# Three gathers of a decoder block leave out the rows of one or two DMA engines; a 48-partition gather brings them, and their steps go last

## The chip, the cores and the metric

The kernel runs on one core of one Trainium2 chip. A core has five engines that run their own instruction streams: TensorE (PE), VectorE (DVE), ScalarE (ACT), GpSimd (POOL) and SyncE (SP). Sixteen DMA engines move data between memory (HBM) and the on-chip SBUF. The metric is the device time of one execution in microseconds; three runs of the kernel before gave a median of 930.43 us (929.78 to 933.73).

## The reference

One layer of a decoder block on 256 tokens of width 1024: an adaptive norm, two attention branches, and a feed-forward part (PEER) that looks up experts. The last part is what matters here. For each token and each of 8 heads the 16 best of 16384 experts are found; each has a row `u` and a row `v` of 1024 numbers.

```python
def one_chunk(args):
    xc, ec, gc = args
    ue = u[ec]
    ve = v[ec]
    act = jax.nn.gelu(jnp.einsum("cd,chkd->chk", xc, ue), approximate=False)
    return jnp.einsum("chk,chkd->cd", (gc * act).astype(ve.dtype), ve)
```

That is 256 x 8 x 16 pairs of rows, 268 MB in float32, gathered from HBM by number. The result is added to the block's stream, and a last norm gives the output.

## The kernel before, in words

The first 237 us load weights and compute the norms and attention for all tokens (for the second half of the tokens the rest of it runs later, between the steps below). Then the expert part runs as 256 steps g, in blocks of 16 (`BLOCK`): one block for each of 8 heads, first for tokens 0 to 127 (steps 0 to 127), then for tokens 128 to 255. In a step each of the 128 partitions is a token, and the step handles one expert of each token. A row of the table `uv` holds `u` and `v` side by side, 2048 float32 or 8 KB.

- POOL issues gather g (L929): an indirect DMA that takes one row number per partition from column g of `expert` and brings 128 rows of 8 KB into slot `SLOT[g]` of eleven. Before it POOL waits until the step that used the slot last (`OLD[g]`) is through: for all late steps that is PE's count `v_used`. At the first gather of a block it also waits for the block's row numbers (`eid_ready`, L1686). The gathers use one semaphore per slot, 16 counts per gather.
- DVE waits for the landing and multiplies the `u` half with the token's row, summing into one number (`dot`, L1711, two instructions).
- ACT makes the step's factor from it (`diagonal`: L1156 the activation, L1165 the gate, L1169 a diagonal 128x128 matrix with the factor).
- PE multiplies that matrix with the `v` half into the sum in PSUM (`value_step`, L808, four matmul instructions of 512 columns in each step, with their weight loads) and counts `v_used`.
- Beside the steps of a block, DVE finds the next block's experts (`halves_first` to `expert_sums` at places 3 to 9 of the block, `normalize` at 11), and ACT its gates (`gate_exponent` at 8).

All engines go through the steps in the same order, 0 to 255. The last two steps (`LAST`, 254 and 255) are gathered in halves of 4 KB: first both `u` halves (L936), then both `v` halves (L939). Step 254 isn't done by PE: DVE multiplies its `v` half by factor and gate (L1830) and adds it to the stream (L1831). Then DVE takes PE's sum in two halves of 512 columns (L1837, L1838; the first half waits for `first_half_done`, set by PE after the first half of step 255), ACT squares and sums them (L1173), and after the root (L1248) DVE scales the rows (L1718) and SP writes them out.

Of the kernel before, what the change touches and what calls it, by code (L numbers as in the profile page):

```python
# [74 lines left out]
for _n, _w in (("ident", P), ("cmask", T), ("cos", TT * HALF), ("sin", TT * 2 * HALF),  # L75
               ("cmp_add", TT * NCMP), ("cmp_mul", TT * NCMP), ("bmask", HEADS), ("pos", NCAND)):
    TAB[_n] = (_at, _at + _w)
    _at += _w
# [48 lines left out]
def transpose_jobs():  # L127
# [18 lines left out]
    for r in (4, 5, 6, 7, 8, 9):  # L146
# [29 lines left out]
EARLY, MORE, MOST = 36, 64, 127  # L176
SLOT = [(0, 1, 2, 3, 4, 5, 6, 9, 10)[g % 9] if g < EARLY else (g - EARLY) % 7 if g < MORE else (7, 8, 0, 1, 2, 3, 4, 5, 6)[(g - MORE) % 9] if g < MOST else
        (9, 10, 7, 8, 0, 1, 2, 3, 4, 5, 6)[(g - MOST) % 11] for g in range(STEPS)]
USE = [SLOT[:g].count(SLOT[g]) for g in range(STEPS)]
OLD = [max((i for i in range(g) if SLOT[i] == SLOT[g]), default=None) for g in range(STEPS)]  # L180

# [3 lines left out]
ON_PE = [v for v in range(STEPS) if v not in ON_DVE and v != STEPS - 2]  # L185
# [17 lines left out]
def build(nc, A, out):  # L203
    with ExitStack() as ctx:
# [25 lines left out]
        last_rows = sb("last_rows", 2 * len(LAST), P, U32)  # L230

# [171 lines left out]
        first_half_done, last_ready, last_amount = sem("first_half_done"), sem("last_ready"), sem("last_amount")  # L403
        last_u = [sem(f"last_u{i}") for i in range(len(LAST))]
# [77 lines left out]
        def _(pe):  # L482
# [317 lines left out]
            def value_step(v):  # L800
# [4 lines left out]
                if v in LAST:  # L805
                    pe.wait_ge(uv_in[SLOT[v]], 16 * (USE[v] + 1))
# [46 lines left out]
            for g in range(STEPS + 1):  # L853
# [3 lines left out]
                if g - 1 in PE_NO and g - 1 >= EARLY_STEPS:  # L857
                    value_step(g - 1)
# [48 lines left out]
        def _(pool):  # L907

            for g in range(STEPS):
# [33 lines left out]
        def _(act):  # L943
# [248 lines left out]
            for g in range(STEPS):  # L1192
                b, i = divmod(g, BLOCK)
                if g >= EARLY_STEPS:
                    diagonal(g)
# [4 lines left out]
                if i == 8 and b + 1 < BLOCKS:  # L1200
# [50 lines left out]
        def _(dve):  # L1251
# [429 lines left out]
            def expert_sums(b, lo, hi):  # L1681
# [5 lines left out]
                dve.wait_ge(eid_ready, b + 2 if b else 1 + lo // 4)  # L1687
                if b == BLOCKS - 1:
# [13 lines left out]
            def dot(g):  # L1702
# [5 lines left out]
                else:  # L1708
                    dve.wait_ge(uv_in[SLOT[g]], 16 * (USE[g] + 1))
# [61 lines left out]
            for g in range(STEPS):  # L1771
# [3 lines left out]
                dot(g)  # L1775
# [173 lines left out]
```

## Time and profile before

| | |
|---|---|
| median of 3 runs | 930.43 us (929.78 to 933.73) |
| profiled execution, its time | 930.88 us |
| its span, first to last instruction | 929.1 us |
| PE busy | 775.1 us, 83% |
| DVE busy | 654.0 us, 70% |
| ACT busy | 413.7 us, 45% |
| POOL busy | 285.8 us, 31% |
| DMA, all bytes | 342.33 MB, mean 368 GB/s over the span |
| first gather issued, last one | 237.3 us, 899.5 us |
| mean granted TensorE clock | 0.98 |

All views come from one execution, the profiled one. Busy shares are means over the whole span; the gathers run in the last three quarters of it. "DMA share" is the time of the DMA packets that begin in a stretch, divided by sixteen engines' time in that stretch; it can come out a little over 1. Times in rows are microseconds from the start of the span unless marked ns; a bracket at the end of a row gives the idle time of the engine before the instruction and what ended it.

### The profile page before, as it was taken

What the parts mean: (1) busy time and instruction counts of PE and PEld (TensorE: products, weight loads), DVE (VectorE), ACT (ScalarE), POOL (GpSimd) and SP (SyncE); (2) the same over time, 40 slices, a digit from 0 to 9 for tenths busy, and PEclk for the clock granted to TensorE, in tenths of its full rate; (3) what the DMA queues carried; (4) which work ended last, traced back from release to release, by engine and by line L of the source; (5) the groups of instructions that cost most, each with busy time, mean ns of one, the idle gap of its engine ahead of it and who ended that gap; (6) DMA issues with size and microseconds to landing.
All of it is one profiled execution on the core that took longest, in us unless ns stands there. A gap on an engine that the chain in (4) does not pass through costs nothing.

```text
span 929.1 us, 9674 instructions
## 1 busy us (share of the span) xinstructions
PE 775.1 (83%) x2880; PEld 418.6 (45%) x2880; DVE 654.0 (70%) x1697; ACT 413.7 (45%) x1157; POOL 285.8 (31%) x262
## 2 busy tenths in 40 slices
PE   4999999998978897897787798778687777877785
PEld 3445778888724453354444364323222222222221
DVE  4534669974798879867666868685966757576656
ACT  3112222342568789342424543564634344353433
POOL 0000000000444344553333445525354252543430
PEclk8999999999999999999999999999899999999999
DMA  9967249660799999999999999999999999999993
GB/s 362 423 260 328 91 158 378 279 273 23 284 423 420 420 393 393 424 420 417 419 420 419 420 418 423 420 422 421 421 424 420 422 422 420 422 420 423 422 420 152
DMA packets 47619, 342.33 MB, mean 368 GB/s; under 512 B 5392, under 2 KB 6608, under 8 KB 11088
## 3 DMA queue, kind: packets, MB, share of 16 engines
q0 software_dynamic: 37152, 268.45, 69.8%
q1 hardware_dynamic: 9968, 72.79, 19.6%
q10 hardware_dynamic: 448, 0.48, 0.2%
q8 instruction: 23, 0.38, 0.2%
q14 instruction: 28, 0.23, 0.1%
HBM read 340.65 MB, written 1.05 MB: 368 GB/s over the span
## 4 chain that ended last, share of the span: by engine, by line
DMA 44%; PE 30%; DVE 13%; ACT 4%; issue 4%; POOL 3%; SPq 0%; POOLq 0%; DVEq 0%
DMA extra<-in_uv,arena 27%; DMA arena<-in_uv,arena 13%; PE banks L808 7%; PE banks L562 6%; PE banks L516 5%; DVE extra L1711 3%; PE banks L525 3%; POOL extra L929 3%; DMA extra<-in_uv,last_rows 2%; PE banks L778 2%; PE banks L759 2%; DMA extra<-in_w_ada 2%; PE banks L747 2%; DVE arena L1711 1%; DVE arena L1730 1%
## 5 line engine op out<-in xcount | busy, mean ns | idle before, releaser
L929 POOL DMA_INDIRECT extra<-in_uv,arena x132 | 150.1, 1137 | 430.2 <-DVE arena L1759 236.9
L808 PE MATMUL banks<-extra 128*128 128x512 f32 x472 | 231.4, 619 | 58.7 <-ACT extra L1169 57.7
L808 PE MATMUL banks<-arena,extra 128*128 128x512 f32 x312 | 156.3, 626 | 40.6 <-ACT extra L1169 40.6
L1156 ACT ACTIVATE arena<-arena 128x1 f32<-128x1 f32 x256 | 51.6, 202 | 305.3 <-DVE arena L1711 304.8
L808 PEld LDWEIGHTS banks<-extra 128*128 128x128 f32 x472 | 82.4, 191 | 184.2 <-ACT extra L1169 114.0
L929 POOL DMA_INDIRECT arena<-in_uv,arena x84 | 93.9, 1118 | 135.3 <-PE banks L808 58.5
L1711 DVE CUSTOM_DVE_ANT_0 extra<-extra 128x1024 f32<-128x1024 f32 x75 | 91.6, 1225 | 36.4 <-DMA extra<-in_uv,arena 35.2
L808 PEld LDWEIGHTS banks<-arena,extra 128*128 128x128 f32 x312 | 54.5, 192 | 130.4 <-ACT extra L1169 84.9
L1711 DVE CUSTOM_DVE_ANT_0 extra<-extra,arena 128x1024 f32<-128x1024 f32 x59 | 72.2, 1225 | 43.7 <-DMA extra<-in_uv,arena 43.1
L1169 ACT ACTIVATE extra<-tab,arena 128x128 f32<-128x128 f32 x234 | 93.9, 401 | 7.7
L808 PE MATMUL banks<-ring,extra 128*128 128x512 f32 x152 | 74.4, 616 | 20.6 <-ACT extra L1169 20.4
L1711 DVE CUSTOM_DVE_ANT_0 arena<-arena 128x1024 f32<-128x1024 f32 x45 | 55.1, 1225 | 37.3 <-DMA arena<-in_uv,arena 36.8
L1165 ACT ACTIVATE arena<-arena 128x1 f32<-128x1 f32 x234 | 68.9, 294 | 7.6
L1711 DVE CUSTOM_DVE_ANT_0 arena<-arena,extra 128x1024 f32<-128x1024 f32 x39 | 47.6, 1225 | 15.2 <-DMA arena<-in_uv,arena 14.6
L808 PEld LDWEIGHTS banks<-ring,extra 128*128 128x128 f32 x152 | 26.5, 191 | 63.3 <-ACT extra L1169 41.3
L929 POOL DMA_INDIRECT ring<-in_uv,arena x38 | 36.9, 970 | 45.8 <-PE banks L808 28.7
L562 PE MATMUL banks<-arena,extra 128*128 128x256 f32 x192 | 46.0, 394 | 0.8 <-ACT arena L1035 0.5
L516 PE MATMUL banks<-arena 128*128 128x512 f32 (+1 forms) x96 | 42.8, 604 | 3.2 <-ACT arena L980 3.2
L1711 DVE CUSTOM_DVE_ANT_0 ring<-ring,arena 128x1024 f32<-128x1024 f32 x24 | 29.4, 1225 | 18.9 <-DMA ring<-in_uv,arena 18.6
L562 PEld LDWEIGHTS banks<-arena,extra 128*128 128x128 f32 x192 | 36.7, 196 | 6.5 <-issue 1.6
L1156 ACT ACT_TABLE_LOAD x30 | 38.5, 1283 | 0.5
L778 PE MATMUL banks<-arena 128*128 128x128 f32 x256 | 33.6, 288 | 3.7 <-ACT arena L1111 3.7
(280 smaller groups left out, 1044.7 us busy)
## 6 DMA issues: line engine op xcount, KB each, us to landing
arena<-in_w_ada SPq DMA_DIRECT2D x6, 2048.0 KB, 8.4
arena<-in_w_late SPq DMA_DIRECT2D x24, 512.0 KB, 8.2
extra<-in_w_ada SPq DMA_DIRECT2D x6, 1024.0 KB, 17.1
extra<-in_w_gate SPq DMA_DIRECT2D x3, 2048.0 KB, 8.3
extra<-in_w_in SPq DMA_DIRECT2D x2, 2048.0 KB, 31.6
extra<-in_w_ada SPq DMA_DIRECT2D x2, 2048.0 KB, 9.8
extra<-in_w_br SPq DMA_DIRECT2D x2, 2048.0 KB, 9.2
arena<-in_w_wq SPq DMA_DIRECT2D x2, 2048.0 KB, 14.5
```

The lines of the kernel that those rows point to most:

```text
L516: last = nc.tensor.matmul(B[2 * c + tt][:, 0:CHUNK_COLS[c]], hT[:, k, tt * P:(tt + 1) * P], first[:, k, c0:c0 + CHUNK_COLS[c]], start=(k = ...
L525: last = nc.tensor.matmul(B[2 * (c - FIRST) + tt][:, 0:CHUNK_COLS[c]], hT[:, k, tt * P:(tt + 1) * P], w[:, k, :], start=(k == 0), stop=(k ...
L562: last = nc.tensor.matmul(B[6 if m else 1][:, 0:T], w[:, k, (m % 4) * P:(m % 4 + 1) * P], hT[:, k, :], start=(k == 0), stop=(k == KT - 1))
L747: last = nc.tensor.matmul(merge_bank[tt][m // 2 % 2][:, (2 * (m % 2) + b) * P:(2 * (m % 2) + b + 1) * P], wb[b][:, k, :], oT[:, b, k, :], ...
L759: last = nc.tensor.matmul(B[m % 2][:, 0:P], w[:, k, :], hT[:, k, tt * P:(tt + 1) * P], start=(k == 0), stop=(k == KT - 1))
L778: last = nc.tensor.matmul(B[m % 2][:, 0:P], w[:, k, :], h2[:, k, tt * P:(tt + 1) * P], start=(k == 0), stop=(k == KT - 1))
L808: last = nc.tensor.matmul(acc[tt][:, half * 512:(half + 1) * 512], diag[i % DIAGS], uv_slot[SLOT[v]][:, D + half * 512:D + (half + 1) * 51 ...
L929: nc.gpsimd.indirect_dma_start(uv_slot[SLOT[g]], None, A["uv"], bass.IndirectOffsetOnAxis(ap=expert[:, g:g + 1], axis=0)).then_inc(uv_in[S ...
L1156: link(nc.scalar.activation(gel[:, v:v + 1], dots[:, v:v + 1], ACT.Gelu))
L1165: link(nc.scalar.activation(amount[:, v:v + 1], gel[:, v:v + 1], ACT.Copy, scale=weight[:, v:v + 1]))
L1169: nc.scalar.activation(diag[i % DIAGS], ident, ACT.Identity, scale=amount[:, v:v + 1]).then_inc(diag_ready, 1)
L1711: V.tensor_tensor_reduce(out=row, in0=row, in1=h2row[g // FIRST_HALF], scale=1.0, scalar=0.0, op0=ALU.mult, op1=ALU.add, accum_out=dots[:, ...
```

## The change

Three gathers, of steps 233, 234 and 235 (`APART`), are told not to fetch some rows: a number of 1048576 (`SKIP`) is added to the row numbers of the partitions concerned, and the gather has a bounds check that passes over numbers beyond the table. Left out are the eight partitions that its formula `engine_rows` gives for DMA engine 3 (12 to 15 and 44 to 47), for step 235 also those of engine 1 (4 to 7 and 36 to 39). A second gather for each, over partitions 0 to 47 alone (`NARROW`), issued by POOL right after gathers 244, 245 and 246, fetches what was left out and passes over the others; POOL waits before it for the first part's landing. The row numbers for both come from two new DVE instructions when block 14's experts are known, with a table of 6 new columns.

The steps 233 to 235 are processed by DVE, ACT and PE after step 253 and before 254 (`ORDER`). Their three slots aren't used again, so that from gather 236 on eight slots go round. Block 15's experts and gates are found three places earlier in block 14, by the count of steps processed. `LANDED` replaces the count of uses in the waits for a landing. The core of the diff:

```diff
+APART = (STEPS - 23, STEPS - 22, STEPS - 21)
+APART_SECOND = {STEPS - 12 + i: c for i, c in enumerate(APART)}
+AHEAD = len(APART)
+NARROW = 48
+SKIP = 1 << 20
+def engine_rows(e):
+    return [p for p in range(P) if 8 * (p >> 6) + ((p >> 2) & 7) == e]
+APART_ROWS = (engine_rows(3), engine_rows(3), engine_rows(1) + engine_rows(3))
...
-        (9, 10, 7, 8, 0, 1, 2, 3, 4, 5, 6)[(g - MOST) % 11] for g in range(STEPS)]
+        (9, 10, 7, 8, 0, 1, 2, 3, 4, 5, 6)[(g - MOST) % 11] for g in range(APART[-1] + 1)]
+SLOT += [SLOT[APART[0] - 11 + AHEAD + i % (11 - AHEAD)] for i in range(STEPS - len(SLOT))]
+LANDED = [16 * sum(1 + (i in APART) for i in range(g + 1) if SLOT[i] == SLOT[g]) for g in range(STEPS)]
+ORDER = [c for c in range(STEPS - 2) if c not in APART] + list(APART) + [STEPS - 2, STEPS - 1]
...
-                if g - 1 in PE_NO and g - 1 >= EARLY_STEPS:
-                    value_step(g - 1)
+                if g - 1 >= EARLY_STEPS and ORDER[g - 1] in PE_NO:
+                    value_step(ORDER[g - 1])
...
+                if g in APART:
+                    i = 2 * APART.index(g)
+                    pool.wait_ge(apart_ready, 1)
+                    nc.gpsimd.indirect_dma_start(uv_slot[SLOT[g]], None, A["uv"],
+                                                 bass.IndirectOffsetOnAxis(ap=apart_rows[:, i:i + 1], axis=0),
+                                                 bounds_check=KEYS * KEYS - 1, oob_is_err=False).then_inc(uv_in[SLOT[g]], 16)
+                    continue
...
+                if g in APART_SECOND:
+                    c = APART_SECOND[g]
+                    i = 2 * APART.index(c) + 1
+                    pool.wait_ge(uv_in[SLOT[c]], LANDED[c] - 16)
+                    nc.gpsimd.indirect_dma_start(uv_slot[SLOT[c]][0:NARROW, :], None, A["uv"],
+                                                 bass.IndirectOffsetOnAxis(ap=apart_rows[0:NARROW, i:i + 1], axis=0),
+                                                 bounds_check=KEYS * KEYS - 1, oob_is_err=False).then_inc(uv_in[SLOT[c]], 16)
...
-                    diagonal(g)
+                    diagonal(ORDER[g])
...
-                if i == 8 and b + 1 < BLOCKS:
+                if i == (8 - AHEAD if b == BLOCKS - 2 else 8) and b + 1 < BLOCKS:
...
+                if b == APART[0] // BLOCK:
+                    apart = eq[:, 0:2 * len(APART)].rearrange("p (g n) -> p g n", n=2)
+                    first = APART[0] % BLOCK
+                    link(V.tensor_tensor(apart, eid[:, first:first + len(APART)].unsqueeze(2).to_broadcast([P, len(APART), 2]),
+                                         table("skip").rearrange("p (g n) -> p g n", n=2), ALU.add))
+                    V.tensor_copy(apart_rows[:, :], eq[:, 0:2 * len(APART)]).then_inc(apart_ready, 1)
+                    dve.wait_ge(apart_ready, 1)
...
-                dot(g)
+                dot(ORDER[g])
...
+                if b == BLOCKS - 2:
+                    i += AHEAD
```

## Rows read from the trace of the kernel before

**Rows 1.** The page: DMA share in 40 slices (tenths); the gathers' queue (packets, MB, share).
```profile
DMA  9967249660799999999999999999999999999993
...
q0 software_dynamic: 37152, 268.45, 69.8%
```

**Rows 2.** Busy time by stretch: from:to, us, engines (instructions), clock, DMA share, GB/s.
```profile
880.00:900.00 20.00, 15.97 (x34) 5.46 (x33) 9.97 (x17) 7.18 (x24) 9.35 (x10) 1.00 1.02 422
```

**Rows 3.** DVE in order of time: start, us, line; dots of 249, 250, 253, 254.
```profile
904.61 1.23 DVE L1711 CUSTOM_DVE_ANT_0 arena<-arena 128x1024 f32<-128x1024 f32 x1 [1.26 <-DMA arena<-in_uv,arena]
...
907.10 1.23 DVE L1711 CUSTOM_DVE_ANT_0 ring<-ring,arena 128x1024 f32<-128x1024 f32 x1 [1.26 <-DMA ring<-in_uv,arena]
...
914.53 1.22 DVE L1711 CUSTOM_DVE_ANT_0 extra<-extra,arena 128x1024 f32<-128x1024 f32 x1 [1.23 <-DMA extra<-in_uv,arena]
...
915.77 1.22 DVE L1711 CUSTOM_DVE_ANT_0 extra<-extra,arena 128x1024 f32<-128x1024 f32 x1
```

**Rows 4.** DMA queues: all packets from 900 to 905; the instruction queue, 895 to 897.
```profile
DMA packets 289, 2.11 MB, mean 421 GB/s; under 512 B 32, under 2 KB 32, under 8 KB 32
...
q8 instruction: 1, 0.02, 3.2%
```

**Rows 5.** Busy time by stretch of 1 us, the end of the gathers.
```profile
911.00:912.00 1.00, 0.50 (x2) 0.13 (x2) 0.00 (x0) 0.75 (x3) 0.00 (x0) 1.00 0.76 307
912.00:913.00 1.00, 1.00 (x3) 0.52 (x4) 0.93 (x1) 0.00 (x0) 0.00 (x0) 1.00 0.55 225
913.00:914.00 1.00, 0.85 (x2) 0.02 (x1) 0.30 (x2) 0.60 (x3) 0.00 (x0) 1.00 0.35 143
914.00:915.00 1.00, 0.65 (x2) 0.41 (x3) 0.47 (x1) 0.30 (x1) 0.00 (x0) 1.00 0.17 70
915.00:916.00 1.00, 1.00 (x4) 0.27 (x2) 0.99 (x3) 0.20 (x1) 0.00 (x0) 1.00 0.13 53
916.00:917.00 1.00, 0.52 (x2) 0.19 (x2) 1.00 (x2) 0.69 (x2) 0.00 (x0) 1.00 0.07 29
...
918.00:919.00 1.00, 0.80 (x2) 0.00 (x0) 0.93 (x3) 0.63 (x3) 0.00 (x0) 1.00 0.06 25
```

**Rows 6.** The chain that ended last, in order of time: start, us, what.
```profile
898.26 20.00 DMA extra<-in_uv,last_rows
...
918.34 1.30 DVE extra L1830
...
919.66 1.24 DVE arena L1831
...
920.92 0.70 DVE arena L1837
```

**Rows 7.** PE in order of time: steps 253 and 255.
```profile
916.81 1.98 PE L808 MATMUL banks<-extra 128*128 128x512 f32 x4 [0.48 <-ACT extra L1169]
...
919.63 1.95 PE L808 MATMUL banks<-extra 128*128 128x512 f32 x4 [0.84 <-DMA extra<-in_uv,last_rows]
```

**Rows 8.** PE in order of time: three steps without a wait between them.
```profile
669.04 5.31 PE L808 MATMUL banks<-extra 128*128 128x512 f32 x12
```

**Rows 9.** POOL in order of time: gathers 240, 241 and 244.
```profile
867.61 0.94 POOL L929 DMA_INDIRECT ring<-in_uv,arena  x1 [9.52 <-DVE arena L1686]
868.85 0.94 POOL L929 DMA_INDIRECT extra<-in_uv,arena  x1 [0.30 <-issue]
...
873.38 0.97 POOL L929 DMA_INDIRECT extra<-in_uv,arena  x1 [0.31 <-issue]
```

**Rows 10.** DVE in order of time: dot 233 and the row numbers of block 15.
```profile
864.93 1.23 DVE L1711 CUSTOM_DVE_ANT_0 extra<-extra,arena 128x1024 f32<-128x1024 f32 x1 [0.25 <-DMA extra<-in_uv,arena]
...
867.16 0.18 DVE L1686 CAST arena<-arena 128x16 uint32<-128x16 f32 x1
```

**Rows 11.** DMA issues: line, engine, operation, count, KB each, us to landing.
```profile
tab<-in_tab ACTq DMA_DIRECT2D x1, 349.0 KB, 3.1
```

**Rows 12.** All transfers from the table of experts, issue to landing.
```profile
DMA to landing us min/median/max: 5.6/18.7/25.2
```

More of the change, by code:

```diff
@@ L176 @@
 EARLY, MORE, MOST = 36, 64, 127
+APART = (STEPS - 23, STEPS - 22, STEPS - 21)
[6 more added lines that the diff above has]
+APART_ROWS = (engine_rows(3), engine_rows(3), engine_rows(1) + engine_rows(3))
+assert max(max(r) for r in APART_ROWS) < NARROW
 SLOT = [(0, 1, 2, 3, 4, 5, 6, 9, 10)[g % 9] if g < EARLY else (g - EARLY) % 7 if g < MORE else (7, 8, 0, 1, 2, 3, 4, 5, 6)[(g - MORE) % 9] if g < MOST else
-        (9, 10, 7, 8, 0, 1, 2, 3, 4, 5, 6)[(g - MOST) % 11] for g in range(STEPS)]
-USE = [SLOT[:g].count(SLOT[g]) for g in range(STEPS)]
+        (9, 10, 7, 8, 0, 1, 2, 3, 4, 5, 6)[(g - MOST) % 11] for g in range(APART[-1] + 1)]
+SLOT += [SLOT[APART[0] - 11 + AHEAD + i % (11 - AHEAD)] for i in range(STEPS - len(SLOT))]
 OLD = [max((i for i in range(g) if SLOT[i] == SLOT[g]), default=None) for g in range(STEPS)]
+LANDED = [16 * sum(1 + (i in APART) for i in range(g + 1) if SLOT[i] == SLOT[g]) for g in range(STEPS)]
+ORDER = [c for c in range(STEPS - 2) if c not in APART] + list(APART) + [STEPS - 2, STEPS - 1]
 SHARE = 6
 ON_DVE = [v for v in range(FIRST_STEPS) if v % SHARE == SHARE // 2]
-ON_PE = [v for v in range(STEPS) if v not in ON_DVE and v != STEPS - 2]
+ON_PE = [v for v in ORDER if v not in ON_DVE and v != STEPS - 2]
 PE_NO = {v: i for i, v in enumerate(ON_PE)}
@@ L230, in build @@
         last_rows = sb("last_rows", 2 * len(LAST), P, U32)
+        apart_rows = sb("apart_rows", 2 * len(APART), P, U32)
         def table(name):
@@ L403, in build @@
         first_half_done, last_ready, last_amount = sem("first_half_done"), sem("last_ready"), sem("last_amount")
+        apart_ready = sem("apart_ready")
         last_u = [sem(f"last_u{i}") for i in range(len(LAST))]
@@ L805, in value_step @@
                 if v in LAST:
-                    pe.wait_ge(uv_in[SLOT[v]], 16 * (USE[v] + 1))
+                    pe.wait_ge(uv_in[SLOT[v]], LANDED[v])
                 for half in range(2):
@@ L1708, in dot @@
                 else:
-                    dve.wait_ge(uv_in[SLOT[g]], 16 * (USE[g] + 1))
+                    dve.wait_ge(uv_in[SLOT[g]], LANDED[g])
                 row = uv_slot[SLOT[g]][:, 0:D]
@@ L1826, in _ @@
             dve.wait_ge(last_amount, 1)
-            dve.wait_ge(uv_in[SLOT[v]], 16 * (USE[v] + 1))
+            dve.wait_ge(uv_in[SLOT[v]], LANDED[v])
             dve.wait_ge(g2row_out, 1)
@@ L1864, in constants @@
     put("bmask", (np.arange(HEADS * NCMP)[:, None] // NCMP == np.arange(HEADS)[None, :]).astype(np.float32))
+    put("skip", np.stack([np.where(np.isin(p, r) == (n == 0), SKIP, 0) for r in APART_ROWS for n in range(2)], 1).astype(np.float32))
     put("pos", np.tile(np.arange(NCAND, dtype=np.float32), (P, 1)))
```

2 lines of the change are left out of this document (1 added, 1 removed).

## The prediction

> **What bounds the kernel now.** I read the page first: the DMA row stands at nine tenths in nearly every slice from the start of the gathers (237 us) to the last slice, and the gathers' queue alone takes 69.8% of sixteen engines' span [rows 1]. So the second reading is not which engine computes most, but how the gather stretch looks in fine: from 880 to 900 us the sixteen DMA engines are at 1.02 of their time and move 422 GB/s, while PE is busy 15.97 of 20 us and DVE 9.97 [rows 2]. One gather is 128 rows of 8 KB; at that rate it takes 2.49 us, and that is the spacing of the dot products: 2.49 us from one to the next, with DVE idle for half of it until the gather lands [rows 3]. Each of the sixteen engines moves 8 rows of a gather (9 packets per engine and gather, one of them small: 289 packets in 5 us, 32 of them small [rows 4]), so a row costs an engine 2.49 / 8 = 0.311 us.
>
> The third reading is the end of the stretch, microsecond by microsecond, with the DMA share times 16 taken as the number of engines that still work: 12.2 from 911 us, 8.8, 5.6, 2.7 (914 to 915), 2.1, 1.1, and 1.0 up to 919 [rows 5]. The engines don't finish together. One works alone from about 916.1 to 919.0; a second stops 2.8 us before it (0.12 us into the stretch from 916); a third at about 914.7 (2.7 less the two late ones), that is 4.3 us before the last. A gather has landed when all sixteen engines are through, so the late engine dates every landing by itself. Its last rows are what the chain of waits hangs on: 20.00 us of DMA, then L1830 at 918.34, L1837 at 920.92 and the output [rows 6].
>
> **What the change removes.** For gathers 233, 234 and 235 the rows of one engine (24 rows, 7.5 us of its time) are skipped, for 235 also those of another (8 rows, 2.5 us). If these are the two late ones, the late one ends 7.5 us earlier, ahead of nearly all; the second by 2.5 us, 5.3 us before today's end; the third, untouched, then dates the landings: 4.3 us earlier. Call this gain G. What G loses again is the work of the three narrow gathers, which move the same 32 rows over again (32 x 0.311 = 10 us of engine time) on other engines. 128 partitions give an engine 8 rows; 48 partitions give it at most 3 of a gather by the same division, so between 0 and 9 rows, 0 to 2.8 us, for one engine in all three. The engines that stop at 911 or 912 can take that and stay ahead of 914.7; those that stop after 913 can't. I take a loss of 0.8 us, a third of the way, since over half of the engines stop before 913 [rows 5]: G = 3.5, with bounds 1.5 (2.8 us on a neighbour of the third) and 5.3. The upper end is for the third engine: a 16 KB fetch of instructions took 1.0 us of one engine at 895 (3.2% of 16 engines over 2 us) [rows 4], and if it sat on that engine and falls elsewhere after the change, G grows by 1.0.
>
 No run here shows either.
>
> **What the change moves, and what it costs.** Steps 233 to 235 go from their place to behind step 253, and this is the half that the description passes over. Each is one dot (1.24 us from one to the next when data is there [rows 3]), three small ACT operations, and four PE matmuls of 512 columns. Today each lies beside 2.49 us of DMA and costs nothing. After the change steps 236 to 253 still wait for their gathers, one per 2.49 us, so the time saved by passing over 233 to 235 is spent waiting for 236; the three land in full long before, but are taken up only when 253 has landed. Let T be the start of dot 253, today 914.53 [rows 3].
> - Today: PE begins step 253 at T + 2.28 (916.81), step 255 at 919.63 when its data lands, and DVE starts L1837 at 920.92 = T + 6.39 [rows 6, 7].
> - After, on PE: back to back a step takes 1.72 us (12 matmuls in 5.31 us, 0.429 apart [rows 8]). 253, 233, 234, 235 take 6.88 us, so 255 starts at T + 9.16, and its first half is done about half of 1.95 us later [rows 7]: T + 10.14.
> - After, on DVE: six dots of 1.24 us (253, 233, 234, 235, 254, 255), then L1830 and L1831 of 1.32 and 1.26 us with the gap behind them: T + 10.0 [rows 3, 6].
> PE is later by a little, so L1837 starts at T + 10.14, 3.75 us later after T than today. The last two half gathers, which land 5.0 us after 253 today, no longer matter: the tail is compute. The output behind L1837 is unchanged. The total is 3.75 - G = **+0.25 us**.
>
> **What I cost at nothing.** The three added issues on POOL are 1.24 us each (0.94 and 0.30 between two [rows 9]); POOL then issues one gather in 2.49 us, so 1.25 us are free per gather. If a bounds check made the issue twice as long, there would still be no queue. The new wait of POOL for the first landing of 233 comes behind gather 244, issued at 873.38 [rows 9], when dot 233 had begun at 864.93 even with the late engine [rows 10]; queued behind it are gathers 245 on, and nobody waits longer. The wait for the new row numbers is for two small DVE operations made 16 steps earlier, 0.18 us each by the nearest row [rows 10], in a step where DVE would have to be full for it to show; as it idles half of the gather's time, a 0.4 us delay is made good by the next step. Block 15's preparation moves up by three positions with ACT's exponent, and shortens POOL's pause before gather 240 (9.52 us [rows 9]); that pause starves no DMA engine today, as the share shows, so nothing is gained. The table grows by 6 columns, 3 KB on 349 KB that landed in 3.1 us [rows 11]: under 0.1 us, at the start.
>
> **The rivals.**
> - *The gain is whole.* The narrow rows fall on early engines, perhaps the third one is relieved too: G = 4.3 to 5.3, so -0.55 to -1.55, 928.9 to 929.9. For it: over half of the engines have 2 us to give. Against it: 32 rows must miss the four or five engines that stop after 913. Chance 0.18.
> - *The late engine is another one.* This ends slower: T stays at 914.53 while the three steps are still taken behind it, so +3.75, 934.2; each skipped row that the narrow gathers put on the late engine adds 0.311, up to 2.8, 937.0. It decides from G under 3.75 on, and is over 0.5% slower once three rows land there. The rows show one late engine and a second, not which partitions they serve, so the trace can't close this and the forecast takes it as a premise. Chance 0.2. The Trainium skill speaks against the change here ("DMA: Bandwidth & Descriptors", Latency and other measured facts: engines 7 and 15 are usually the slower ones, whose partitions the change doesn't touch; by that the time would be this rival's).
> - *It doesn't do what it says*: skipped rows are moved anyway, to nowhere. Then no engine is relieved and each narrow gather costs all of them 3 rows, 2.8 us in all: +6.55, 937.0. No row speaks for it. Chance 0.02.
> - *Too few buffers.* From 236 on, eight slots go round and not eleven. A slot is free again 4.3 us after its landing (2.28 to PE, 1.98 of PE), so a gather has 8 x 2.49 - 4.3 = 15.6 us from issue to landing, and the first engines, some 4 us ahead of the one that dates the landing, 11.6; the shortest landing in the trace is 5.6 [rows 12]. It would have to double to bite. Some +3, 933.4. Chance 0.03.
>
> **How the numbers follow.** The profiled execution took 930.88 us (span 929.1 and 1.8 around it); with +0.25 it is 931.13. It lies 0.45 over the median of the three runs, 930.43, so against the median the forecast is 930.7. Its chance is 0.57, with a range of its own from 929.9 to 932.7 (G from 4.3 down to 1.5). The range of 8 in 10 adds the gain in full (928.9) and the other engine with up to two narrow rows on it (934.8). Faster or slower by over 0.5% is 4.65 us, about what a measurement can tell from no change: faster would need G over 8.4, all sixteen engines through by 910.6 where 12 of them still work after 911: 0.02. Slower needs the other engine with three narrow rows on it (a quarter of that rival), or rows that are moved anyway, or a part of the last rival: 0.08. The same: 0.9.
>
> **What would show it.** In the profile after: the share of the last microseconds should fall from 1.0 to nothing within some 3 us, without the long step of one engine; the gap between two dots should be near 0 for the last five, with PE at 1.72 us a step; L1830 and PE's last step should wait for no DMA; DVE should stand idle some 2 to 4 us ahead of dot 236. If dot 253 starts at 914.5 again, the wrong engine was skipped; if it starts before 910, G was underestimated. The forecast fails if the three late steps run anywhere but behind 253, or if PE's 1.72 us doesn't hold there.

## The result, and the profile after

The changed kernel took 943.73 us (median of 6 runs, 940.52 to 949.11) against 930.42 us (6 runs, 928.05 to 933.73) for the kernel before on the same chip: 1.0146 times as long, with a 95% interval from 1.0111 to 1.0181. The forecast was 930.7 us, with a range up to 934.8; the kernel is slower by 13.3 us. The profiled execution of the changed kernel took 943.89 us (span 941.7), 13.01 us more than that of the kernel before. (Lines have moved: L1711, L1830, L1837, L808 and L929 of before are L1752, L1873, L1880, L828 and L956 here; in the experiments with one line more, L1753, L1874, L1881, L829 and L957; in e4 and e10 with three more, L1755 and L1883.)

I began where the forecast said that the gain should appear, at dot 236. This is DVE in order of time after the change (start, us, line; the bracket is the idle time before and what ended it), with dots 236 and 239, then 242 to 245 and 247, then 253, and the line that takes PE's sum:

```profile
867.42 1.23 DVE L1752 CUSTOM_DVE_ANT_0 arena<-arena 128x1024 f32<-128x1024 f32 x1 [3.44 <-DMA arena<-in_uv,arena]
...
874.88 1.23 DVE L1752 CUSTOM_DVE_ANT_0 ring<-ring,arena 128x1024 f32<-128x1024 f32 x1 [1.25 <-DMA ring<-in_uv,arena]
...
882.32 1.23 DVE L1752 CUSTOM_DVE_ANT_0 extra<-extra,arena 128x1024 f32<-128x1024 f32 x1 [1.23 <-DMA extra<-in_uv,arena]
...
884.79 1.23 DVE L1752 CUSTOM_DVE_ANT_0 extra<-extra,arena 128x1024 f32<-128x1024 f32 x1 [1.24 <-DMA extra<-in_uv,arena]
...
887.60 1.23 DVE L1752 CUSTOM_DVE_ANT_0 arena<-arena 128x1024 f32<-128x1024 f32 x1 [1.58 <-DMA arena<-in_uv,arena]
...
892.66 1.23 DVE L1752 CUSTOM_DVE_ANT_0 arena<-arena 128x1024 f32<-128x1024 f32 x1 [3.83 <-DMA arena<-in_uv,arena]
...
902.81 1.23 DVE L1752 CUSTOM_DVE_ANT_0 ring<-ring,arena 128x1024 f32<-128x1024 f32 x1 [3.60 <-DMA ring<-in_uv,arena]
...
918.05 1.23 DVE L1752 CUSTOM_DVE_ANT_0 arena<-arena 128x1024 f32<-128x1024 f32 x1 [1.22 <-DMA arena<-in_uv,arena]
...
933.59 0.69 DVE L1880 TENSOR_TENSOR arena<-banks,arena 128x512 f32<-128x512 f32 x1 [4.30 <-PE banks L828]
```

Dots 236 and 242 in the kernel before:

```profile
872.32 1.22 DVE L1711 CUSTOM_DVE_ANT_0 arena<-arena 128x1024 f32<-128x1024 f32 x1 [0.74 <-DMA arena<-in_uv,arena]
...
887.21 1.23 DVE L1711 CUSTOM_DVE_ANT_0 extra<-extra,arena 128x1024 f32<-128x1024 f32 x1 [1.25 <-DMA extra<-in_uv,arena]
```

The gain is there at first: dot 236 starts at 867.42, where the kernel before has it at 872.32, 4.9 us later. At dot 242 the lead still is 4.9 us. From 242 to 247 the five gathers take 20.49 us, where five of 2.485 us, the spacing of [rows 3], would take 12.43: 8.1 us are lost, and the gain with them. Dot 253 (T in the forecast) comes at 918.05, 3.5 us later than before, and L1880 at T + 15.54, where the kernel before needs T + 6.39 [rows 3, 6] and the forecast had T + 10.14. So 3.5 us of the 13.0 are lost by dot 253, 9.15 between it and L1880, and 0.3 outside the span (2.2 us around it, where the kernel before has 1.8).

The stretches of 2 us (to read as [rows 2]: the last two numbers are DMA share and GB/s) show the stretch in which the lead goes. Before the change the stretches from 882 to 894 have 414 to 426 GB/s; one of them, then four after the change:

```profile
886.00:888.00 2.00, 1.49 (x5) 0.52 (x4) 0.79 (x1) 0.89 (x3) 0.00 (x0) 1.00 1.02 422
```

```profile
880.00:882.00 2.00, 2.00 (x4) 0.91 (x3) 1.09 (x2) 0.81 (x3) 0.77 (x1) 0.50 0.81 332
882.00:884.00 2.00, 2.00 (x5) 0.81 (x4) 1.23 (x2) 0.46 (x3) 1.70 (x2) 0.81 0.75 197
...
886.00:888.00 2.00, 2.00 (x5) 0.68 (x4) 0.42 (x3) 0.90 (x3) 1.70 (x2) 1.00 0.95 205
...
890.00:892.00 2.00, 1.87 (x4) 0.56 (x4) 0.00 (x0) 0.00 (x0) 1.70 (x2) 1.00 1.11 299
```

There are two different faults in it. At 880 to 884 the engines have too little to do (share 0.81 and 0.75). From 886 to 896 they are busy nearly all the time (0.89 to 1.13) and yet move only 205 to 377 of their 422 GB/s. The second follows the narrow gathers. The first follows a pause of POOL, and its cause is on ACT; POOL's gathers 243 and 244, and ACT's factor of step 236:

```profile
866.73 0.94 POOL L956 DMA_INDIRECT extra<-in_uv,arena  x1 [1.05 <-PE banks L828]
881.23 0.94 POOL L956 DMA_INDIRECT arena<-in_uv,arena  x1 [13.56 <-PE banks L828]
```

```profile
876.15 0.20 ACT L1190 ACTIVATE arena<-arena 128x1 f32<-128x1 f32 x1 [11.72 <-DVE arena L1752]
```

Dot 236 ends at 868.65, but ACT starts on it at 876.15, when dot 239 (874.88 + 1.23) is done. The reason stands in the code, in a line that the diff leaves as it was: `diagonal(v)` begins with `act.wait_ge(u_used, v + 1)`, a wait for as many dots as the step's own number asks for. As long as steps were processed by number, that was right. Now step 236 is the 234th to be processed and needs 234 dots, and ACT waits for 237. From 236 to 253 ACT, and PE behind it, work three dots behind DVE.

The wait costs PE its clock as well. These are PE's first three steps from 236 on, and a stretch in which they run (the third number from the end is the granted clock):

```profile
877.18 8.18 PE L828 MATMUL banks<-arena,extra 128*128 128x512 f32 x12 [10.72 <-ACT extra L1203]
```

```profile
878.00:880.00 2.00, 2.00 (x4) 0.77 (x3) 0.74 (x3) 0.90 (x3) 0.00 (x0) 0.50 1.03 430
```

PE had been idle for 10.72 us, and from 870 to 882 its granted clock stands at 0.50, the lower of its two levels (1.2 GHz). Three steps take 8.18 us, where three take 5.31 in [rows 8]. Gather 244 waits for the first of them and is issued 4.05 us after its start; in e1 below, at 1.00 (2.4 GHz), it is 2.26 us.

At the end PE has three more steps left when dot 253 is done, because its factors came three dots late. This is PE in order of time; 920.34 is the start of step 250, two steps to a row, 932.46 that of step 255:

```profile
920.34 3.70 PE L828 MATMUL banks<-extra 128*128 128x512 f32 x8 [0.47 <-ACT extra L1203]
923.88 3.60 PE L828 MATMUL banks<-arena,extra 128*128 128x512 f32 x8
927.31 3.60 PE L828 MATMUL banks<-extra 128*128 128x512 f32 x8
930.74 1.88 PE L828 MATMUL banks<-arena,extra 128*128 128x512 f32 x4
932.46 1.88 PE L828 MATMUL banks<-ring,extra 128*128 128x512 f32 x4
```

Seven steps (250 to 253, 233 to 235) lie between T + 2.29 and T + 14.41, 1.73 us each. The forecast had four of them there. In the kernel before there is one [rows 7].

### The profile page after: what moved, and what is told of

Same layout as the page of the kernel before. It is cut to its first block, busy times and chain, and to the rows that moved or that the text cites. A ratio compares the mean times of both kernels' runs of the same rounds, so it can differ in the third digit from the quotient of the medians.

```text
span 941.7 us, 9688 instructions
## 1 busy us (share of the span) xinstructions
PE 778.4 (83%) x2880; PEld 420.8 (45%) x2880; DVE 653.7 (69%) x1699; ACT 412.9 (44%) x1157; POOL 293.6 (31%) x265
## 3 DMA queue, kind: packets, MB, share of 16 engines
q0 software_dynamic: 37344, 268.45, 69.6%
HBM read 341.84 MB, written 1.05 MB: 364 GB/s over the span
## 4 chain that ended last, share of the span: by engine, by line
DMA 42%; PE 31%; DVE 14%; issue 5%; ACT 4%; POOL 3%; SPq 0%; DVEq 0%
DMA arena<-in_uv,arena 16%; DMA ring<-in_uv,arena 15%; DMA extra<-in_uv,arena 9%; PE banks L828 8%; PE banks L582 5%; PE banks L536 5%; PE banks L545 3%; DVE extra L1752 2%; PE banks L798 2%; PE banks L767 2%; DVE arena L1752 2%; DMA extra<-in_w_ada 2%; PE banks L779 2%; POOL arena L956 1%; DVE ring L1752 1%
## 5 line engine op out<-in xcount | busy, mean ns | idle before, releaser
L956 POOL DMA_INDIRECT extra<-in_uv,arena x129 | 147.5, 1143 | 430.4 <-DVE arena L1800 235.7
L828 PE MATMUL banks<-extra 128*128 128x512 f32 x464 | 227.7, 620 | 55.1 <-ACT extra L1203 54.8
L828 PE MATMUL banks<-arena,extra 128*128 128x512 f32 x316 | 161.6, 639 | 51.7 <-ACT extra L1203 51.7
L828 PEld LDWEIGHTS banks<-extra 128*128 128x128 f32 x464 | 81.6, 191 | 176.5 <-ACT extra L1203 106.3
L956 POOL DMA_INDIRECT arena<-in_uv,arena x84 | 94.8, 1129 | 150.3 <-PE banks L828 75.2
L828 PEld LDWEIGHTS banks<-arena,extra 128*128 128x128 f32 x316 | 57.0, 197 | 144.7 <-ACT extra L1203 95.0
L1752 DVE CUSTOM_DVE_ANT_0 extra<-extra 128x1024 f32<-128x1024 f32 x75 | 91.5, 1224 | 35.7 <-DMA extra<-in_uv,arena 34.6
L1752 DVE CUSTOM_DVE_ANT_0 extra<-extra,arena 128x1024 f32<-128x1024 f32 x56 | 68.4, 1224 | 42.7 <-DMA extra<-in_uv,arena 42.2
L828 PE MATMUL banks<-ring,extra 128*128 128x512 f32 x156 | 78.4, 631 | 22.7 <-ACT extra L1203 22.7
L1752 DVE CUSTOM_DVE_ANT_0 arena<-arena 128x1024 f32<-128x1024 f32 x47 | 57.5, 1225 | 43.0 <-DMA arena<-in_uv,arena 42.4
L1752 DVE CUSTOM_DVE_ANT_0 arena<-arena,extra 128x1024 f32<-128x1024 f32 x39 | 47.6, 1224 | 16.6 <-DMA arena<-in_uv,arena 15.9
L828 PEld LDWEIGHTS banks<-ring,extra 128*128 128x128 f32 x156 | 27.7, 193 | 66.1 <-ACT extra L1203 43.1
L956 POOL DMA_INDIRECT ring<-in_uv,arena x38 | 38.6, 1015 | 34.8 <-PE banks L828 27.7
L1752 DVE CUSTOM_DVE_ANT_0 ring<-ring,arena 128x1024 f32<-128x1024 f32 x25 | 30.6, 1226 | 21.2 <-DMA ring<-in_uv,arena 20.9
L798 PEld LDWEIGHTS banks<-arena 128*128 128x128 f32 x256 | 32.1, 200 | 7.8 <-issue 7.2
```

What stands on the lines that cost most here:

```text
L798: last = nc.tensor.matmul(B[m % 2][:, 0:P], w[:, k, :], h2[:, k, tt * P:(tt + 1) * P], start=(k == 0), stop=(k == KT - 1))
L828: last = nc.tensor.matmul(acc[tt][:, half * 512:(half + 1) * 512], diag[i % DIAGS], uv_slot[SLOT[v]][:, D + half * 512:D + (half + 1) * 51 ...
L1752: V.tensor_tensor_reduce(out=row, in0=row, in1=h2row[g // FIRST_HALF], scale=1.0, scalar=0.0, op0=ALU.mult, op1=ALU.add, accum_out=dots[:, ...
```

## The experiments

All times are medians. "Lead" is how much earlier a dot starts than in the kernel before's trace, "slip" what the gathers 243 to 247 take over 5 x 2.485 us. The traces aren't level to begin with: at dot 224, ahead of everything that the change moves, they are up to 6.4 us apart, and nearly as far at dot 150. A table behind the experiments gives each lead from that origin.

**The waits of ACT mended (e1).** Everything of the change, but ACT counts places.

```diff
+PLACE = {c: i for i, c in enumerate(ORDER)}
...
-                act.wait_ge(u_used, v + 1)
+                act.wait_ge(u_used, PLACE[v] + 1)
```

> The changed kernel with one wait mended: ACT's factor of a step waits for as many dot products as the step's place in ORDER asks for, where the changed kernel still asks for the step's number (three more from step 236 on). Theory W (this count held ACT, PE and with them the slots back by three gathers, 7.5 us, and eight slots then ran dry): the loss goes and the forecast's own sum holds, +0.25 us on the kernel before, 930.7 (928.9 to 932.7), and POOL's pause of 13.56 us before gather 244 is gone. Rival N (the narrow gathers are slow on the chip by themselves: packets of 8 KB took up to 1.2 us around them): 938 to 944. Rival B (eight slots are too few even with the right count): 938 to 944, with POOL's pause still above 8 us.

938.08 us against 929.87 before (1.0102, interval 1.0063 to 1.0142). By the medians the wait is worth 5.65 us, or 5.1 if each is taken over the kernel before beside it, which was 0.55 us faster here; 8.2 remain. DVE, dots 242, 243, 245, 247 and 253, and the line that takes PE's sum:

```profile
882.26 1.23 DVE L1753 CUSTOM_DVE_ANT_0 extra<-extra,arena 128x1024 f32<-128x1024 f32 x1 [1.25 <-DMA extra<-in_uv,arena]
...
885.10 1.22 DVE L1753 CUSTOM_DVE_ANT_0 extra<-extra,arena 128x1024 f32<-128x1024 f32 x1 [1.60 <-DMA extra<-in_uv,arena]
...
892.68 1.23 DVE L1753 CUSTOM_DVE_ANT_0 arena<-arena 128x1024 f32<-128x1024 f32 x1 [3.33 <-DMA arena<-in_uv,arena]
...
900.51 1.23 DVE L1753 CUSTOM_DVE_ANT_0 ring<-ring,arena 128x1024 f32<-128x1024 f32 x1 [1.87 <-DMA ring<-in_uv,arena]
...
915.40 1.23 DVE L1753 CUSTOM_DVE_ANT_0 arena<-arena 128x1024 f32<-128x1024 f32 x1 [1.25 <-DMA arena<-in_uv,arena]
...
925.78 0.69 DVE L1881 TENSOR_TENSOR arena<-banks,arena 128x512 f32<-128x512 f32 x1 [0.96 <-PE banks L829]
```

The tail is now T + 10.38, as forecast within 0.24 us. The lead of 4.95 us at dot 242 is lost all the same: a slip of 18.25 - 12.43 = 5.8 us, and dot 253 is 0.9 us late. POOL pauses 4.06 us before gather 244, not 13.56, and no stretch from 882 to 898 has a share under 0.91 any more. What stays are full engines with little moved (two stretches of e1):

```profile
884.00:886.00 2.00, 1.50 (x5) 0.68 (x4) 0.90 (x1) 0.46 (x2) 0.93 (x1) 1.00 1.04 266
...
890.00:892.00 2.00, 1.60 (x4) 0.68 (x4) 0.00 (x0) 0.35 (x1) 1.09 (x2) 1.00 0.91 213
```

**The order alone, without the skipped rows (e2 and e3).** Whole gathers for 233 to 235 and no second ones; e2 with ACT's wait mended, e3 with the wait as the change has it.

```diff
-APART_SECOND = {STEPS - 12 + i: c for i, c in enumerate(APART)}
+APART_SECOND = {}
-LANDED = [16 * sum(1 + (i in APART) for i in range(g + 1) if SLOT[i] == SLOT[g]) for g in range(STEPS)]
+LANDED = [16 * sum(1 for i in range(g + 1) if SLOT[i] == SLOT[g]) for g in range(STEPS)]
...
-                if g in APART:
+                if False:
```

> The reordering alone, with the mended wait: gathers 233 to 235 bring all rows, there is no narrow gather, the three steps are still taken last and their slots are not used again. Theory W: only the tail counts, +3.75 us by the forecast's sum, 934.2 (933 to 935.5), with dot 253 at the same time as in the kernel before. Rival B (eight slots too few): 938 or more. Rival N says nothing on it.

> The reordering alone, with the wait as the changed kernel has it: whole gathers, no narrow ones. Theory W: a slot is free 4.3 + 7.5 = 11.8 us after its landing, so 8 x 2.49 - 11.8 = 8.1 us are left from issue to landing for the late engine and nothing for the first ones, which are 8 us ahead of it; the queue runs dry as in the changed kernel, and with the tail's 3.75 us it is as slow or slower: 940 to 947. Rival N: without narrow gathers nothing is slow but the tail, 934.

e2: 936.47 us (1.0078, 1.0048 to 1.0108). Dot 253 starts at 913.13 and PE's sum is taken at 923.52, T + 10.39. The 4.0 us of the tail are there without any skipped row. The median lies 6.6 us over the kernel before, more than 4.0; its four runs go from 933.81, the profiled one, to 936.85. The three slower ones have a lower mean granted clock too (0.966 to 0.970 against 0.972), as slower runs of the kernel before have (934.11 us at 0.966, 927.50 at 0.979); which of the two brings the other isn't shown.

e3: 942.77 us (1.0141, 1.0111 to 1.0172), as slow as the change itself, which has the skipped rows besides. Dot 253 starts at 919.32, and L1880 at 934.85, T + 15.53. The late count so costs 5.15 us behind dot 253 whether rows are skipped or not. It starves the queue too; three stretches of e3, in the first of which PE (first number after the stretch's length) is still idle, after its last matmul ended at 869.5, and its granted clock is at 0.50:

```profile
882.00:884.00 2.00, 0.00 (x0) 0.00 (x0) 1.23 (x2) 0.13 (x1) 0.00 (x0) 0.50 0.99 414
884.00:886.00 2.00, 1.10 (x2) 0.58 (x3) 0.93 (x1) 0.77 (x3) 0.00 (x0) 0.50 0.61 254
886.00:888.00 2.00, 2.00 (x4) 0.92 (x3) 0.79 (x3) 0.90 (x3) 0.00 (x0) 0.50 0.20 82
```

**The late count alone, in the kernel before (e8).** The order and the gathers of before, eleven slots, and ACT made to wait for three more dots from step 233 to 250.

```diff
-                act.wait_ge(u_used, v + 1)
+                act.wait_ge(u_used, v + 4 if 233 <= v < 251 else v + 1)
```

> The kernel before, with one thing added: in steps 233 to 250 ACT's factor waits for three more dot products than it needs, as it does in the changed kernel. Order, gathers and all eleven slots stay. Theory S (the wait costs because eight slots less three leave the queue too short): with eleven slots less three, the first engines have about 7 us from issue to landing, over the shortest landing of 5.6, so nothing runs dry and the end is as before, 930 (929 to 932). Rival A (the wait alone costs the 5.6 us that lie between the changed kernel and the one with the mended wait): 935 to 936.

935.12 us against 929.64 (1.0053, 1.0031 to 1.0076). From dot 236 to 253 the dots stay 2.44 to 2.50 us apart, so with eleven slots going round the late count doesn't starve the engine that dates them; the loss is at PE, which I had overlooked in what I expected. DVE's dot 253 and the taking of PE's sum:

```profile
919.50 1.23 DVE L1711 CUSTOM_DVE_ANT_0 extra<-extra,arena 128x1024 f32<-128x1024 f32 x1 [1.20 <-DMA extra<-in_uv,arena]
...
929.89 0.69 DVE L1837 TENSOR_TENSOR arena<-banks,arena 128x512 f32<-128x512 f32 x1 [2.59 <-PE banks L808]
```

T + 10.39 and not T + 6.39: three steps more behind dot 253, by another way. The time is Rival A's, 935 to 936, and Theory S was right only on the queue. (T itself is 5 us late in this profile, and so is dot 224; only the distance from T is used.)

**The rows skipped and never fetched (e5).** e1 without the second gathers; 32 rows of steps 233 to 235 are left out.

```diff
-APART_SECOND = {STEPS - 12 + i: c for i, c in enumerate(APART)}
+APART_SECOND = {}
-LANDED = [16 * sum(1 + (i in APART) for i in range(g + 1) if SLOT[i] == SLOT[g]) for g in range(STEPS)]
+LANDED = [16 * sum(1 for i in range(g + 1) if SLOT[i] == SLOT[g]) for g in range(STEPS)]
```

> The changed kernel with the mended wait, without the three narrow gathers: the 32 rows are skipped and never fetched (this part of the computation is left out; the steps use what lay in the slots). Theory C (the narrow gathers hold up all sixteen engines, and that ate the gain): the gain G of 4.8 us, seen at step 242, lasts to dot 253, which starts near 909.7; with the tail's 4.0 us the whole is 0.8 us faster than before, 929 (927.5 to 931). Rival B (the late engine's gain is lost by itself, by eight slots or by other engines falling back): dot 253 later than 912 and 932 or more.

930.26 us against 930.10 (0.9998, 0.9974 to 1.0021). Dot 253, the taking of PE's sum, and the stretch that had 213 GB/s in e1:

```profile
909.84 1.23 DVE L1753 CUSTOM_DVE_ANT_0 arena<-arena 128x1024 f32<-128x1024 f32 x1 [1.25 <-DMA arena<-in_uv,arena]
...
920.22 0.69 DVE L1881 TENSOR_TENSOR arena<-banks,arena 128x512 f32<-128x512 f32 x1 [0.96 <-PE banks L829]
```

```profile
890.00:892.00 2.00, 1.50 (x4) 0.49 (x3) 0.75 (x3) 0.90 (x3) 1.70 (x2) 1.00 1.00 418
```

Here the lead lasts: dot 253 is 4.7 us earlier than before, of which 0.7 were there at dot 224, so 4.0 are gained by skipping. (It is 5.1 from dot 239 to 248; dot 249 comes 1.1 us late, at 899.90, and a 0.02 MB packet of the instruction queue began between 897.0 and 897.5. The prediction had put such a fetch at 1.0 us of one engine; that it is the cause here isn't shown.) The tail takes 10.38, 4.0 more than before, and gives them back, as the medians say. This is the forecast's kernel, with the narrow gathers at no cost; even it isn't faster.

**The same rows brought back by the late engine itself (e7).** e1 with second gathers over all 128 partitions, by the formula of the change again engines 3 and 1.

```diff
-NARROW = 48
+NARROW = 128
```

> The changed kernel with the mended wait; the second gathers are over 128 partitions and not 48, so that the rows come through the same engine that was spared, later. Theory P: no jam, because one engine writes its own group; the late engine gets its 24 rows back, dot 253 where it was (914.5) and the tail's 4.0 us on top: 934 (933 to 936.5). Rival F (skipped rows or the bounds check make the second gather slow): 938 or more, with stretches under 300 GB/s.

934.08 us against 930.10 (1.0054, 1.0032 to 1.0075). DVE, dots 245 to 247, and a stretch of 2 us:

```profile
888.37 1.23 DVE L1753 CUSTOM_DVE_ANT_0 arena<-arena 128x1024 f32<-128x1024 f32 x1 [1.62 <-DMA arena<-in_uv,arena]
...
893.33 1.23 DVE L1753 CUSTOM_DVE_ANT_0 arena<-arena 128x1024 f32<-128x1024 f32 x1 [3.73 <-DMA arena<-in_uv,arena]
...
898.29 1.23 DVE L1753 CUSTOM_DVE_ANT_0 ring<-ring,arena 128x1024 f32<-128x1024 f32 x1 [3.73 <-DMA ring<-in_uv,arena]
```

```profile
890.00:892.00 2.00, 1.35 (x3) 0.68 (x4) 0.00 (x0) 0.56 (x2) 0.94 (x1) 1.00 1.02 422
```

Each of the gathers 246 and 247 comes 4.96 us after the one before, twice 2.48: eight rows of the gather and eight of the one that was postponed. The slip is 5.3 us, hardly less than e1's 5.8, and no stretch from 882 to 898 is below 406 GB/s. So most of the slip is not the doing of the narrow form. Dot 253 starts at 913.14, where e2 has 913.13 (at dot 224 they are 0.2 us apart): skipping the rows and bringing them back later is worth nothing.

**Two rows per gather (e9), rows of eight groups (e6).** If other engines have time to spare, a few rows should cost the late one nothing. e9 skips two partitions of the late group in each gather; e6 skips one partition of each of eight groups (for 235 two of each).

```diff
-APART_ROWS = (engine_rows(3), engine_rows(3), engine_rows(1) + engine_rows(3))
+APART_ROWS = ([12, 44],) * 3
```

```diff
-APART_ROWS = (engine_rows(3), engine_rows(3), engine_rows(1) + engine_rows(3))
+EIGHT = list(range(0, 32, 4))
+APART_ROWS = (EIGHT, EIGHT, EIGHT + [p + 1 for p in EIGHT])
```

> The changed kernel with the mended wait, but each of the three gathers leaves out two rows alone (partitions 12 and 44 of the late engine's eight), and each narrow gather brings two. Theory K (what jams is several engines writing into the late engine's eight partitions at once, so two rows at a time do little): no stretch of 2 us under 390 GB/s, the late engine ends 6 rows or 1.9 us earlier, dot 253 some 1.9 us earlier relative to the start of the stretch, the tail costs 4.0: +2.1, 932. Rival P (these eight partitions take no more than one engine's rate whoever writes, so each row comes back as 0.31 us): +4.0, 934. Rival F (any narrow gather jams): +6 or more, 936.

> The changed kernel with the mended wait, but the rows left out and brought later belong to eight engines, one row each (two each for step 235), and not all to one or two; the narrow gathers have the same form, the same number of rows and the same place. Theory P (rows of one group of eight partitions, written by several engines at once, jam the transfers of all): no jam, landings of 244 to 247 stay 2.49 us apart, no 2 us under 380 GB/s; the late engine gives up 4 rows, 1.2 us, the tail costs 4.0: +2.8, 932.7 (931 to 935). Rival F (a narrow gather with skipped rows is slow whatever its rows): stretches of 200 to 300 GB/s as with the mended wait alone, 938.

e9: 933.76 us against 929.64 (1.0062, 1.0036 to 1.0089). DVE, dots 241 to 245:

```profile
881.35 1.23 DVE L1753 CUSTOM_DVE_ANT_0 extra<-extra,arena 128x1024 f32<-128x1024 f32 x1 [1.25 <-DMA extra<-in_uv,arena]
...
884.16 1.23 DVE L1753 CUSTOM_DVE_ANT_0 extra<-extra,arena 128x1024 f32<-128x1024 f32 x1 [1.58 <-DMA extra<-in_uv,arena]
...
887.26 1.23 DVE L1753 CUSTOM_DVE_ANT_0 extra<-extra,arena 128x1024 f32<-128x1024 f32 x1 [1.87 <-DMA extra<-in_uv,arena]
...
890.37 1.23 DVE L1753 CUSTOM_DVE_ANT_0 arena<-arena 128x1024 f32<-128x1024 f32 x1 [1.87 <-DMA arena<-in_uv,arena]
...
893.17 1.23 DVE L1753 CUSTOM_DVE_ANT_0 arena<-arena 128x1024 f32<-128x1024 f32 x1 [1.57 <-DMA arena<-in_uv,arena]
```

The gathers 242 to 245 take 11.82 us, 1.88 over 4 x 2.485: six rows of 0.31 us, all that had been skipped. One by one the four gathers take about 0.32, 0.62, 0.62 and 0.32 us too long, as one, two, two and one rows would make them. The place says something on who moves them. In e7, where the late engine should have the postponed rows in its own queue behind gathers 244 to 246, gathers 245 to 247 come late. In e9 the delay already falls on 242 to 244, before the late engine could have reached the second gathers, if it takes its queue in order as e7 suggests. So, I conclude, engines that are some gathers ahead move these rows, and the late one, whose gathers are in hand then, loses 0.31 us for each; no view names the engines. Dot 253 starts at 913.06, again that of e2.

e6: 935.95 us against 930.10 (1.0056, 1.0036 to 1.0077). Its lowest stretch:

```profile
896.00:898.00 2.00, 1.08 (x4) 0.25 (x2) 0.86 (x2) 0.90 (x3) 0.00 (x0) 1.00 1.01 303
```

From 890 to 900 it has 303 to 389 GB/s at a share of 1.01 to 1.05. So the hold-up is there although each row belongs to another group (for 235 two to a group), which Theory P had excluded: it isn't a matter of rows crowding into one group alone.

**The steps taken in between (e4), and the three mends together (e10).** e4 is e1 with steps 233 to 235 taken behind 246, 249 and 251; e10 also has the second gathers over 128 partitions (NARROW = 128, as in e7).

```diff
-ORDER = [c for c in range(STEPS - 2) if c not in APART] + list(APART) + [STEPS - 2, STEPS - 1]
+AFTER = {246: 233, 249: 234, 251: 235}
+ORDER = [c for s in range(STEPS) if s not in APART for c in ((s, AFTER[s]) if s in AFTER else (s,))]
```

> The changed kernel with the mended wait, and the three steps taken behind steps 246, 249 and 251 and not behind 253. Theory W with the forecast's sum: their dots, factors and matmuls lie beside the gathers again, so the 3.75 us of the tail go and G stays: 930.4 - 3.5 = 926.9 (925.5 to 929). Rival N: 934 or more, since the narrow gathers stay. If dot 253 starts near 910 but the end doesn't come earlier, PE was still behind.

> The changed kernel with the three other edits together: ACT's wait counts places, steps 233, 234 and 235 are taken behind 246, 249 and 251, and the second gathers go over 128 partitions, so that the late engine itself brings its rows back. If the three costs found so far (the stale count, the tail, the hold-up of all sixteen engines) are all there is, what is left is the late engine's total work, which is that of before: the time is e7's less 4.0 us of tail, 930.1 us, within 0.3% of before; dot 253 starts at 913 to 914.5 and DVE takes PE's sum 6.4 us behind it. If the order in which rows are fetched is worth anything by itself, dot 253 starts by 910 and the time is under 927. If the rows through other engines cost nothing beyond their own 0.31 us, it is no better than e4, 932.3.

e4: 932.25 us against 929.87 (1.0029, 1.0007 to 1.0051): the tail's cost is gone, as Theory W had it, but no gain is left, as it had not. e10: 931.35 us against 930.05 (1.0009, 0.9991 to 1.0028), which can't be told from before. DVE's dot 253 and the taking of PE's sum, first e4, then e10:

```profile
914.71 1.23 DVE L1755 CUSTOM_DVE_ANT_0 arena<-arena 128x1024 f32<-128x1024 f32 x1 [1.24 <-DMA arena<-in_uv,arena]
...
921.07 0.69 DVE L1883 TENSOR_TENSOR arena<-banks,arena 128x512 f32<-128x512 f32 x1
```

```profile
914.62 1.23 DVE L1755 CUSTOM_DVE_ANT_0 arena<-arena 128x1024 f32<-128x1024 f32 x1 [1.19 <-DMA arena<-in_uv,arena]
...
920.98 0.69 DVE L1883 TENSOR_TENSOR arena<-banks,arena 128x512 f32<-128x512 f32 x1
```

Both are back at T + 6.36, so the tail goes away when the steps are taken where DVE and PE are idle; nothing takes its place. And T is 914.71 and 914.62, where the kernel before has 914.53 [rows 3]. In e10, where stale count, tail and narrow form are gone, the skipped rows still bring no time. No version beats the kernel before.

**All leads from dot 224 on.** The kernel before starts it at 842.44 us. The first column is the lead that a profile already has at dot 224, the others what has come to it by dots 236 and 253 (us).

| | lead at 224 | gained by 236 | gained by 253 |
|---|---|---|---|
| the change | 0.33 | 4.57 | -3.85 |
| e1, count mended | 0.11 | 4.85 | -0.98 |
| e2, whole gathers | 1.35 | 0.05 | 0.05 |
| e3, whole gathers, late count | -2.92 | 0.09 | -1.87 |
| e4, taken in between | 1.01 | 4.87 | -1.19 |
| e5, never fetched | 0.73 | 5.54 | 3.96 |
| e6, eight groups | -6.35 | 1.25 | -1.17 |
| e7, second gathers over 128 | 1.58 | 5.12 | -0.19 |
| e8, late count in the kernel before | -5.06 | 0.04 | 0.09 |
| e9, two rows | 1.55 | 1.85 | -0.08 |
| e10, three mends | 0.15 | 4.93 | -0.24 |

The leads at 236 follow the rows that the late group is spared, until another engine dates the landing: four rows in e6 give 1.25 us, six in e9 1.85, twenty-four 4.6 to 5.5. By 253 all is repaid in e7, e9 and e10, and about 1 us more in e1, e4 and e6, the versions whose engines are held up.

## Why the prediction was wrong, point by point

**What bounds the kernel: right.** One engine dates the landings and serves the partitions that the change skips: the gain at dot 236 is 4.6 us from dot 224 on, within the bounds 1.5 to 5.3, and e5 keeps 4.0 to the end. The rival of another late engine falls. With it falls, for this kernel, what I had weighed from the Trainium skill ("DMA: Bandwidth & Descriptors", Latency and other measured facts: engines 7 and 15 are usually the slower ones): the rows skipped were those of engine 3 by the page's own formula, and the gain came. That skipped rows are moved after all falls too (e5).

**The three steps behind 253: right, 4.0 us.** Forecast 3.75; T + 10.38 or 10.39 in e1, e2, e5, e7 and e9, and gone in e4 and e10, where the steps stand elsewhere.

**The step that failed first: "What G loses again is the work of the three narrow gathers, which move the same 32 rows over again on other engines".** I took 0.8 us for it, which I called a third of 2.8 (that would be 0.9), and 2.8 as its most, counting the rows per engine that moves them. It cost 5.3 us in e7 and 5.8 in e1, the whole lead. The count has to go by the partitions that receive: eight partitions get the same rows in either kernel, and they come at 0.31 us each whichever engine brings them (e7: 4.96 us for sixteen of them; e9: 1.88 us for six). If so, the late engine is not late for lack of hands, and another engine can't help it; a skipped row is a loan. That the loan is repaid in full is shown (e7, e9, e10); that the receiving side sets the rate is concluded from where e9's delay falls. The Trainium skill states the cause that fits ("SBUF — State Buffer", Door 1: The DMA port swizzle): partitions 12 to 15 and 44 to 47 share one of sixteen ports, 27.2 GB/s each, by which 8 KB would take 0.30 us as an estimate. The measured 0.31 agrees, but doesn't decide: one engine by itself also takes 2.49 / 8 = 0.31 us for a row. I hadn't weighed that section.

**The step that cost most, a wait put at nothing: ACT's.** The list of what costs nothing holds POOL's new waits and leaves out this old one. "Each is one dot, three small ACT operations, and four PE matmuls" moved the steps as if every engine followed the new order. ACT's count didn't. It costs 5.15 us in the tail (T + 15.54 against T + 10.38; e3 against e2 the same) and, by draining the queue, 2.2 us of slip (8.06 in the change, 5.83 in e1), 2.9 by dot 253. In medians it is 5.65 us (the change against e1) and 6.3 (e3 against e2). The prediction asked who is queued behind each new wait, but not which old wait counts steps by their number.

**The sum.** Forecast: 3.75 - 3.5 = +0.25. Measured in the profile, step by step: tail 4.0, no gain where 3.5 was due and 0.98 lost besides (e1 by dot 253), late count 5.15 behind T and 2.87 ahead of it (3.85 - 0.98), 0.34 outside the span, less the 0.33 that the profile was ahead at dot 224: 4.0 + 0.98 + 5.15 + 2.87 + 0.34 - 0.33 = 13.0.

**Too few buffers** was given .03 and +3 us. With the order alone it doesn't bite (e2: POOL pauses 10.8 us before gather 244 and the dots from 236 to 253 stay 2.44 to 2.50 us apart). With the late count, which keeps each slot three dots longer, it does (share 0.75 in the change, 0.20 in e3).

**Still open.** The hold-up of the engines costs about 1 us by the table: e1 loses 0.8 more than e7, e4 0.95 more than e10, e6 1.1 more than e9. That is one profile each; the medians of e4 and e10 differ by 0.9 us, but their intervals (1.0007 to 1.0051 and 0.9991 to 1.0028) overlap, and those of e1 and e7, which ran on two chips, by 4.0, more than the table explains. Why the packets get slow, and which engines carry a 48-partition gather, no view here says.

## What to carry to other kernels

Where one DMA engine dates every landing, count the bytes that its partitions get in all, not those of one gather: here postponing them only lent time, through other engines too, and the lead must be looked for at the end of the stretch, behind the repayment. When steps are reordered, list every wait in all engines that is a function of the step's number, the unchanged lines above all; one of them cost more here than what the change meant to gain. And a step moved behind the last gather costs its full length there, even if it was free where it stood.

## What the runs showed of the hardware

Second gathers of eight to sixteen rows over 48 partitions hold up the engines as a whole: in e1, from 882 to 898, the share stays at 0.91 to 1.13 while 213 to 389 GB/s are moved, and in e7, with the same rows in second gathers over 128 partitions, 406 to 426. With two rows at a time (e9) no stretch from 882 to 898 falls under 406, though six rows still cost 1.88 us. With rows of eight groups (e6) the hold-up is there again, down to 303. The packets themselves get slow: of those of 8 KB that begin after 865 us, 216 took over 0.4 us in e1, up to 1.24, and 114 in e6, but 2 each in e5, e7, e10 and the kernel before. The 16 in e9 are no more than in e2, which has no second gathers. In e3, whose queue had run dry, there are 78 without any second gather, so these are not the only way to it. The Trainium skill tells of something alike for another path ("DMA: Bandwidth & Descriptors", Back-pressure in remote DMA: a saturated destination port backs up to the source engines and to those that share the path). That it is the same mechanism in gathers from HBM isn't shown, and e6, whose rows go to eight groups, doesn't fit one saturated port.

A skipped row isn't quite nothing: the gathers' queue has 37344 packets after the change, 192 more than before [rows 1], with the same 268.45 MB; and in e5, which never fetches 32 rows, as many packets as before, with 0.26 MB less, which is 32 x 8 KB. First after the change, then e5:

```profile
q0 software_dynamic: 37344, 268.45, 69.6%
```

```profile
q0 software_dynamic: 37152, 268.19, 69.7%
```

Of the 192, 3 x 16 would be one small packet for each engine in each of the three second gathers, as [rows 4] shows them for every gather; that leaves 144, which is 3 x 48, the rows of the second gathers, of which only 32 are fetched. So a row that is passed over still counts as a packet, without its 8 KB; e5 shows it directly, with 5424 packets under 512 B where the kernel before has 5392, 32 more.
